# A decoder step on one core: the entry of the gate stage, with its first weights loaded earlier and one gate block kept out of memory

## The chip, the cores and the metric

The kernel is one program on one core of a Trainium2 chip. Its time is the device time of one execution in microseconds (us); of several runs the median counts. The engines that matter are TensorE (PE, matrix products; PEld are its weight loads), VectorE (DVE), ScalarE (ACT) and GpSimd (POOL). SyncE (SP) issues most transfers, and the transfers themselves are carried by the DMA engines. Each engine works through its own instructions in order and waits for others at semaphores.

## The reference, cut to what matters

One decoder layer for 1024 prompt tokens and 8 x 4 sample tokens, T = 1056 columns in all, with a model width of 1024, in float32:

```python
h = rmsnorm(x, w['norm1_g'])
proj = h @ w['w_in']
a_uv, pool_in, qkv, f_raw, z, xbc, dt_raw, gate_raw = jnp.split(proj, split_points, axis=-1)
...        # four branches: gated MLP y_a, pooling y_b, attention y_c, state scan y_d (256 wide each)
merged = jnp.zeros_like(x)
for i, y_i in enumerate((y_a, y_b, y_c, y_d)):
    gate = jax.nn.sigmoid(gate_raw[..., i * D_MODEL:(i + 1) * D_MODEL])
    merged = merged + gate * (y_i.astype(adt) @ w['w_branch'][i])
x = x + merged @ w['w_out']
...        # then a convolved feed-forward layer and the final norm
```

Branch D is a chunked scan over the prompt, with a carried state, and one stored state for each of the 8 sample sequences (`ssd_chunked`, called with `h0`). Its output goes through a norm before it is merged.

## The kernel before, in words

Everything is kept transposed: 128 channels on the partitions, the 1056 tokens along the free side, in three chunks of 352. A product is done in three parts for precision: each operand is split into a high part (a copy rounded to the matmul's type) and a low part (the rest), and high x high, low x high and high x low are summed. One block of 128 output channels over an input of 1024 is 8 steps x 3 parts x 3 chunks = 72 matmuls. Weights are loaded by SP into two buffers `w_raw`, and GpSimd splits each block (`split`, L897: a mark, a copy to `w_hi`, a subtraction to `w_lo`). The y tensors are split by ScalarE (`y_hi`) and VectorE (`y_lo`).

The stretch that the change touches runs like this.

*Early gate blocks.* The gates of branches 0 and 1 (16 blocks, `NE`) are computed in pieces of 9 matmuls between the small matmuls of the attention (6 blocks), of the scan (8 blocks) and of the sample states (2 blocks, `STATE_FILL` = 2 pieces for each of 8 states). TensorE sums a block in PSUM buffer `ps[1]`; ScalarE copies it out and stores it to `gate_raw` in device memory (L1178, L1179). The gates of branches 2 and 3 are computed later, one block each per merge round.

*The scan.* In step c of 9, VectorE multiplies the decays into the score matrix (`seg`, L1756), TensorE uses it (L2306), VectorE takes the results, and then prepares the decays of the next step (L1730, L1732). GpSimd does the step's state products (the last is `xte`, L961) and then the split of a weight block. After the decays of the last step VectorE makes 16 copies into `ctm` (L1782), which the sample states' matmuls read.

*The sample states.* For each of 8 states: GpSimd makes a masked copy (`xtm`, L970, in the buffers `c_s` and `nc_s`), TensorE multiplies it (L2352), transposes the next old state (L2343), does the filling pieces (L2144) and the outputs (L2362). VectorE builds the new state (L1743); SP then loads the state after next (L756) and stores the new one (L758).

*The merge stage.* In round j of 8, for 128 output channels: a gate block of branch 2, branches 0 and 2 (18 matmuls each, L2408), a gate block of branch 3, branches 1 and 3. The order of branches is `BRANCHES` = (0, 2, 1, 3), and their sums lie in `ps` 1, 0, 0, 1. Gates of branches 0 and 1 are loaded back from `gate_raw` into `sgl` (which lies in `cst`) and get their sigmoid there (L1274); those of 2 and 3 get it from PSUM into `sg` (L1283). VectorE multiplies and adds (L1818, L1820). In round 0 the first gate block is interleaved with the transposes of branch D's nine tiles (L2379), which VectorE moves out (L1803). The memory of the scan is then free (`free_of_s1`), and only then may the branch weights be loaded and `y_hi` and `y_lo` be written, in the order of the channels 0 to 7 (L1287, L1809).

The weights of round 0 come late in SP's order: behind the loads and stores of all states,

```python
        sp.wait_ge(h_sent[0], 16 * 5)
        sp.wait_ge(h_sent[1], 16 * 4)
...
        load_gate_weights(0, 0)
        load_gate_weights(0, 1)
        free_of_s1(sp)
```

Of the kernel before, what the change touches and what calls it, by code (L numbers as in the profile page):

```python
# [22 lines left out]
F32 = mybir.dt.float32  # L23
# [6 lines left out]
P = 128  # L30
# [18 lines left out]
FH = 2  # L49
NE = 16  # L50
EA = 6
# [117 lines left out]
def decoder_layer(nc, a, o):  # L169

    top = ExitStack()
    gate_raw = nc.dram_tensor("gate_raw", (NE, P, T), F32, kind="Internal").ap()

# [3 lines left out]
    def sem(name):  # L177
        return top.enter_context(nc.semaphore(name))
# [93 lines left out]
    N1B = len(JOBS)  # L272
    early = [("eg", g, COL_GATE + (g % 2) * D + (g // 2) * P) for g in range(NE)]
    JOBS += early[:EA]
# [19 lines left out]
    ATT_FILL = [(1, 1) if qb < NT // 2 else (1, 0) for qb, h in steps]  # L294
    SSD_LEAD, SSD_FILL, STATE_FILL = 2, [(3, 3)] + [(4, 4)] * (NT - 1), 2

# [212 lines left out]
    ld_sg, sl_ready = sem("ld_sg"), sem("sl_ready")  # L509
    BRANCHES, BRANCH_PS = (0, 2, 1, 3), (1, 0, 0, 1)  # L510
    merged_used = sem("merged_used")
    EARLY_H2 = 2
# [11 lines left out]
    y_sent = [sem(f"y_sent{n}") for n in range(3)]  # L524
    W3 = N1F
    W4 = W3 + 2 * KD
# [79 lines left out]
    def _(sp):  # L606
# [142 lines left out]
        for c in range(NT):  # L749
            load_early(ssd_blocks[c][1])  # L750

        for b in range(NB + 2):
            if b >= 2:
                sp.wait_ge(h_ready, b - 1)
            if b < NB:
                sp.dma_start(h0[b % 2][:, :, :], by_pair(a["state_ssd"][0, b])).then_inc(ld_h0[b % 2], 16)  # L756
            if b >= 2:
                sp.dma_start(by_pair(o["ssd_sample"][0, b - 2]), h_out[b % 2]).then_inc(h_sent[b % 2], 16)  # L758
# [21 lines left out]
        def load_gate_weights(j, s):  # L780

            load_block(W3, s, 2, j, w_in[:, :, bass.ds(at(j * P + (COL_GATE + (2 + s) * D)), P)])

        load_gate_weights(0, 0)
        load_gate_weights(0, 1)
        free_of_s1(sp)
        for n in range(2):
            sp.wait_ge(e_sent[n], 16 * (NE // 2))
        load_branch(0, 0)
        load_branch(0, 1)  # L790
        load_gate(0, 0)
        with sp.Fori(1, KD) as j:
# [87 lines left out]
    def _(gp):  # L880
# [85 lines left out]
        for b in range(NB):  # L966
            split_early(state_blocks[b - 1] if b >= 1 else ssd_blocks[-1][1])
            if b >= 2:
                pt_filled(gp, ("sn", b - 2))
            od.run(g.tensor_scalar(xtm[b % 2][:, :], xte[NT % 2][0:NS].rearrange("p h d -> p (h d)"),  # L970
                                   const("bsel", slice(0, NS), slice(b, b + 1)), None, ALU.mult), xtm_done)

        def split_block(base, q, per, i):
# [5 lines left out]
        def split_gate(j, s):  # L979

            gp.wait_ge(gate_full, j * 2 + (s - 1))
            split_block(W3, s, 2, j)

# [9 lines left out]

        gp.wait_ge(e_full, NE - 1)
        split_block(W3, 0, 2, 0)
        gp.wait_ge(e_full, NE)
        split_block(W3, 1, 2, 0)
        free_of_s1(gp)
        split_branch(0, 0)
        split_branch(0, 1)  # L1000
        od.peel()
        with gp.Fori(1, KD) as j:
# [63 lines left out]
    def _(act):  # L1066
# [104 lines left out]
        def evacuate_early(blocks):  # L1171

            nonlocal n_early
            while n_early < blocks:
                act.wait_ge(e_full, n_early + 1)
                if n_early >= 2:
                    act.wait_ge(e_sent[n_early % 2], 16 * (n_early // 2))
                od.run(sc.activation(in_chunks(gst[n_early % 2]), chunked(1), ACT.Copy), (e_free, n_early + 1))  # L1178
                act.dma_start(gate_raw[n_early], gst[n_early % 2]).then_inc(e_sent[n_early % 2], 16)  # L1179
                n_early += 1  # L1180
# [90 lines left out]
        def gate_loaded(j, s):  # L1271

            act.wait_ge(ld_sg, j * 32 + 16 * (s + 1))
            od.run(sc.activation(sgl, sgl, ACT.Sigmoid), sl_ready)  # L1274
# [10 lines left out]
        free_of_s1(act)  # L1285
        for b in range(KD):
            od.run(sc.activation(y_hi[:, b, :], y_all[:, b, :], ACT.Copy), y_hi_done)  # L1287
        od.peel()
        gate_loaded(0, 0)
        gate_computed(0, 0)  # L1290
        gate_loaded(0, 1)
        gate_computed(0, 1)
        with act.Fori(1, KD) as j:
            od.enter(j, 1)
            gate_loaded(j, 0)
            gate_computed(j, 0)
            gate_loaded(j, 1)
            gate_computed(j, 1)
# [110 lines left out]
    def _(dve):  # L1409
# [339 lines left out]
        for c in range(NT + 1):  # L1749
# [25 lines left out]
            if c + 1 <= NT:  # L1775
                decays(c + 1)
            if c == NT - 1:

                dve.wait_ge(d_zeroed, 1)
                for g in range(2):  # L1780
                    for b in range(NB):
                        od.run(v.tensor_copy(ctm[:, g, b, b * NQ:(b + 1) * NQ], xc[:, 4 + g, SEQ + b * NQ:SEQ + (b + 1) * NQ]),  # L1782
                               ctm_done)
                for b in range(NB):
                    new_state(b)
# [10 lines left out]
        for t in range(NT + 1):  # L1796
            r = rows_of(t)
            key = ("yd", t)
            if t == 0:
                for n in range(2):  # L1800
                    dve.wait_ge(e_sent[n], 16 * (NE // 2))
            pt_filled(dve, key)
            od.run(v.tensor_tensor(y_all[:, 6:8, t * P:t * P + r],  # L1803
                                   pt_of(key)[:, 0:256].rearrange("p (b t) -> p b t", b=2)[:, :, 0:r],
                                   pv[:, PV_SG:PV_SG + 2].unsqueeze(2).to_broadcast([P, 2, r]), ALU.mult), ptf_of(key))

        for b in range(KD):
            dve.wait_ge(y_hi_done, b + 1)
            od.run(v.tensor_tensor(y_lo[:, b, :], y_all[:, b, :], y_hi[:, b, :].bitcast(F32), ALU.subtract), y_split)  # L1809
# [138 lines left out]
    def _(pe):  # L1948
# [433 lines left out]
        def gate(j, s, between=None):  # L2382
            n = W3 + s
            pe.wait_ge(w_split, j * 2 + (n + 1))
            if isinstance(j, int) and s == 0:
                pe.wait_ge(ps0_free, NST + NT + 1)
            else:
                pe.wait_ge(br_read, j * 4 + (2 * s - 1))
            product(ps[s], n % 2, between).then_inc(gate_full, 1)

        def branch(j, p):
            q = BRANCHES[p]
            pe.wait_ge(b_split, j * 4 + (p + 1))
            if isinstance(j, int):
                pe.wait_ge(y_split, 2 * q + 2)
            if p % 2 == 1:
                pe.wait_ge(sg_ready, j * 2 + (p // 2 + 1))
            elif p == 2:
                pe.wait_ge(br_read, j * 4 + 2)
            elif isinstance(j, int):  # L2400
                pe.wait_ge(e_free, NE)
            else:
                pe.wait_ge(br_read, j * 4)
# [8 lines left out]
        def merge_round(j, between=None):  # L2412
            gate(j, 0, between)
            branch(j, 0)
            branch(j, 1)
            gate(j, 1)
            branch(j, 2)
            branch(j, 3)
# [168 lines left out]
```

## Time and profile before

| | us |
|---|---|
| runs shown | 1977.64, 1973.81, 1972.26 |
| their median | 1973.81 |
| the profiled execution's own time | 1970.56 |
| its span, from first to last instruction | 1968.8 |
| TensorE busy in it | 1870.7 (95%) |
| VectorE busy | 892.4 (45%) |
| ScalarE busy | 412.1 (21%) |
| GpSimd busy | 575.3 (29%) |

The profile is of one execution. TensorE is busy almost always, and 88% of the chain of work that ended last is TensorE's. So the time is what TensorE has to do, at the clock that it is granted, and the gaps in which it waits. The waits list who waited for whom; the timeline lists instructions in the order of time, and in brackets behind a row is the idle time before it and what ended it.

### The profile page before, as it was taken

To read this page: it belongs to the slowest core of one execution; us is meant where nothing else is said; L and a number is where in the kernel's file an instruction comes from. 1 tells how busy PE (TensorE), PEld (TensorE's weight loads), DVE (VectorE), ACT (ScalarE), POOL (GpSimd) and SP (SyncE) were. 2 spreads that over 40 slices of the span, in tenths; PEclk is the share of its full clock that TensorE was granted. 3 is DMA by queue.
4 is the path that set the end of the run, shared out by engine and by line. 5 is a ranking of instruction groups with operands and counts; after the bars stand their busy time and mean duration, and the time that the engine had idled before them with its cause. 6 is when DMAs were issued, how large, how long until landed. Compare 5 with 4: busy or idle time off the path is not lost.

```text
span 1968.8 us, 29869 instructions
## 1 busy us (share of the span) xinstructions
PE 1870.7 (95%) x11562; PEld 1795.2 (91%) x11562; DVE 892.4 (45%) x1359; ACT 412.1 (21%) x591; POOL 575.3 (29%) x532
## 2 busy tenths in 40 slices
PE   5899899999999878999999999999999999999997
PEld 4899887888899868999999989999999999999986
DVE  5763334435533325222232255555555554555555
ACT  5211123423411112111121132112111111111223
POOL 2223211022233323333331223324323432432420
PEclk9899999999999889999999999999999999999998
DMA  4121311012222122222223311112111111111202
GB/s 123 45 52 38 87 45 44 12 60 65 60 65 68 55 78 68 70 80 81 81 62 85 98 44 44 43 33 64 43 32 53 44 41 43 53 43 32 64 11 97
DMA packets 156098, 113.44 MB, mean 58 GB/s; under 512 B 10742, under 2 KB 146651, under 8 KB 155990
## 3 DMA queue, kind: packets, MB, share of 16 engines
q1 hardware_dynamic: 153084, 102.61, 18.4%
q10 hardware_dynamic: 2940, 9.81, 1.3%
q8 instruction: 51, 0.84, 0.2%
q14 instruction: 23, 0.19, 0.0%
HBM read 95.37 MB, written 16.99 MB: 57 GB/s over the span
## 4 chain that ended last, share of the span: by engine, by line
PE 88%; DVE 7%; ACT 1%; DMA 1%; issue 1%; POOL 1%; ACTq 0%; SPq 0%; DVEq 0%; POOLq 0%
PE ps L1959 17%; PE ps L1965 16%; PE ps L1962 16%; PE ps L2144 10%; PE ps L2408 4%; PE pt L2505 4%; PE pt L2507 4%; PE pt L2506 4%; PE ps L2188 2%; PE ps L2126 2%; PE ps L2445 1%; PE pt L2176 1%; DVE y_lo L1809 1%; DMA w_raw<-in_w_in 1%; DVE ext L1863 1%
## 5 line engine op out<-in xcount | busy, mean ns | idle before, releaser
L1959 PE MATMUL ps<-h_hi,w_hi 128*128 128x352 f32 x2088 | 458.7, 328 | 26.6 <-POOL w_lo L901 16.8
L1965 PE MATMUL ps<-h_hi,w_lo 128*128 128x352 f32 x2088 | 452.5, 324 | 0.0
L1962 PE MATMUL ps<-h_lo,w_hi 128*128 128x352 f32 x2088 | 452.0, 325 | 0.0
L1959 PEld LDWEIGHTS ps<-h_hi,w_hi 128*128 128x128 f32 x2088 | 355.2, 190 | 29.9 <-POOL w_lo L901 17.5
L894 POOL TENSOR_TENSOR mark<-eps 128x1 f32<-128x1 f32 x159 | 44.4, 279 | 1134.3 <-PE ps L1965 503.0
L1965 PEld LDWEIGHTS ps<-h_hi,w_lo 128*128 128x128 f32 x2088 | 360.2, 189 | 0.0
L1962 PEld LDWEIGHTS ps<-h_lo,w_hi 128*128 128x128 f32 x2088 | 357.0, 189 | 0.0
L901 POOL TENSOR_TENSOR w_lo<-w_raw,w_hi 128x1024 fp32r<-128x1024 f32 x127 | 332.4, 2617 | 10.2
L1897 DVE TENSOR_TENSOR y_all<-y_all,pt 128x352 f32<-128x352 f32 x264 | 137.5, 521 | 113.8 <-PE pt L2507 110.9
L2505 PE MATMUL pt<-act_hi,w_hi 128*128 128x352 f32 x528 | 172.4, 327 | 7.4 <-DVE y_all L1897 6.9
L2507 PE MATMUL pt<-act_hi,w_lo 128*128 128x352 f32 x528 | 170.6, 323 | 0.0
L2506 PE MATMUL pt<-act_lo,w_hi 128*128 128x352 f32 x528 | 170.0, 322 | 0.0
L1877 DVE SCALAR_TENSOR_TENSOR cv<-ext,pv,cv 128x1072 f32<-128x1072 f32 x88 | 144.7, 1644 | 11.9 <-DVE cv L1877 0.2
L900 POOL CAST w_hi<-w_raw 128x1024 fp32r<-128x1024 f32 x127 | 132.9, 1046 | 0.0
L1353 ACT ACTIVATE cv<-ext,pv 128x1072 f32<-128x1072 f32 x44 | 56.5, 1285 | 305.6 <-DVE ext L1866 305.6
L2505 PEld LDWEIGHTS pt<-act_hi,w_hi 128*128 128x128 f32 x528 | 99.3, 188 | 11.7 <-DVE y_all L1897 10.7
L2506 PEld LDWEIGHTS pt<-act_lo,w_hi 128*128 128x128 f32 x528 | 99.4, 188 | 0.0
L2507 PEld LDWEIGHTS pt<-act_hi,w_lo 128*128 128x128 f32 x528 | 99.1, 188 | 0.0
L1863 DVE TENSOR_TENSOR ext<-ps,cst 128x704 f32<-128x704 f32 x44 | 39.2, 892 | 125.4 <-PE ps L1965 125.2
L1363 ACT ACTIVATE act_hi<-cv 128x1024 fp32r<-128x1024 f32 (+1 forms) x44 | 28.4, 645 | 310.1 <-DVE cv L1883 309.4
L2144 PE MATMUL ps<-h_hi,w_hi 128*128 128x352 f32 x384 | 90.1, 343 | 0.2 <-ACT y_all L1178 0.2
L2144 PE MATMUL ps<-h_lo,w_hi 128*128 128x352 f32 x384 | 84.6, 329 | 0.0
(341 smaller groups left out, 2112.5 us busy)
## 6 DMA issues: line engine op xcount, KB each, us to landing
w_raw<-in_w_in SPq DMA_DIRECT2D x52, 512.0 KB, 4.2
w_raw<-in_ffn_up SPq DMA_DIRECT2D x44, 512.0 KB, 3.9
w_raw<-in_ffn_down SPq DMA_DIRECT2D x22, 512.0 KB, 3.6
gate_raw<-y_all ACTq DMA_DIRECT2D x16, 528.0 KB, 2.7
cst<-gate_raw SPq DMA_DIRECT2D x16, 528.0 KB, 3.6
x_tok<-in_x_prompt SPq DMA_DIRECT2D x8, 512.0 KB, 4.1
bw_raw<-in_w_branch SPq DMA_DIRECT2D x32, 128.0 KB, 3.5
w_raw<-in_w_out SPq DMA_DIRECT2D x8, 512.0 KB, 5.0
```

The costliest lines, as they stand in the source:

```text
L900: od.run(g.tensor_copy(hi, raw))
L901: od.run(g.tensor_tensor(lo, raw, hi.bitcast(F32), ALU.subtract), w_split)
L1877: od.run(v.scalar_tensor_tensor(cv[k][:, 0:w], x[:, j:j + w], pv[:, bass.ds(blk + (PV_FW + 2 * NFF * j), 1)], cv[k][:, 0:w], ALU.mult, ALU ...
L1897: od.run(v.tensor_tensor(dst, dst, pt[n % 2][:, 0:CH], ALU.add), dn_done)
L1959: mm(dst[:, c, 0:CH], f_hi[n][:, k, :], h_hi[:, k, tok], start=k == 0, stop=False)
L1962: mm(dst[:, c, 0:CH], f_hi[n][:, k, :], h_lo[:, k, tok], start=False, stop=False)
L1965: last = mm(dst[:, c, 0:CH], f_lo[n][:, k, :], h_hi[:, k, tok], start=False, stop=k == KD - 1)
L2144: last = mm(ps[1][:, c, 0:CH], w[n % 2][:, k, :], h[:, k, c * CH:(c + 1) * CH], start=k == 0 and m == 0, stop=k == KD - 1 and m == 2)
L2408: last = mm(ps[BRANCH_PS[p]][:, c, 0:CH], w[p % 2][:, k, :], y[:, 2 * q + k, c * CH:(c + 1) * CH], start=k == 0 and n == 0, stop=k == 1 an ...
L2505: mm(dst, w[:, m, :], act_hi[:, k, tok], start=k == 0, stop=False)
L2506: mm(dst, w[:, m, :], act_lo[:, k, tok], start=False, stop=False)
L2507: last = mm(dst, w_rest[:, m, :], act_hi[:, k, tok], start=False, stop=k == 1)
```

## The change

Five edits belong together:

1. The weights of the first gate block of branch 2 and of one gate block of branch 0 are loaded before the sample states' loads (SP), and split among and right behind the masked copies (GpSimd). The weights of the first gate block of branch 3 follow behind the states.
2. One of the 16 early gate blocks (the first of branch 0) is no longer computed among the states and stored. There are 15 early blocks, and each state has one filling piece in place of two. The kept block is computed in round 0 behind the first gate block, summed in `ps[1]`, and ScalarE takes its sigmoid straight from there. The early blocks are now in the order branch 1, 0, 1, ... 
3. GpSimd's masked copies no longer stand behind a split: a split now stands behind the second of them.
4. VectorE's 16 copies into `ctm` move from the last scan step to step 2, behind the decays of step 3.
5. `y_hi` and `y_lo` are written in the order of the branches (channels 0, 1, 4, 5, 2, 3, 6, 7). Behind the first four, ScalarE does the sigmoids of the first gate block and of the kept block, then the last four.

```diff
-NE = 16
+NE = 15
...
-    early = [("eg", g, COL_GATE + (g % 2) * D + (g // 2) * P) for g in range(NE)]
+    early = [("eg", g, COL_GATE + ((g + 1) % 2) * D + ((g + 1) // 2) * P) for g in range(NE)]
...
-    SSD_LEAD, SSD_FILL, STATE_FILL = 2, [(3, 3)] + [(4, 4)] * (NT - 1), 2
+    SSD_LEAD, SSD_FILL, STATE_FILL = 2, [(3, 3)] + [(4, 4)] * (NT - 1), 1
...
+    Y_ORDER = [2 * q + k for q in BRANCHES for k in range(2)]
...
-    W3 = N1F
+    W3 = N1F + 1
...
+        for n, col in ((N1F, COL_GATE + 2 * D), (N1F + 1, COL_GATE)):
+            load_block(n, 0, 2, 0, w_in[:, :, col:col + P])
+
         for b in range(NB + 2):
...
-        load_gate_weights(0, 0)
         load_gate_weights(0, 1)
         free_of_s1(sp)
...
         load_branch(0, 0)
         load_branch(0, 1)
-        load_gate(0, 0)
...
         for b in range(NB):
-            split_early(state_blocks[b - 1] if b >= 1 else ssd_blocks[-1][1])
             if b >= 2:
                 pt_filled(gp, ("sn", b - 2))
             od.run(g.tensor_scalar(xtm[b % 2][:, :], xte[NT % 2][0:NS].rearrange("p h d -> p (h d)"),
                                    const("bsel", slice(0, NS), slice(b, b + 1)), None, ALU.mult), xtm_done)
+            if b == 1:
+                split_job(N1F)
...
-        gp.wait_ge(e_full, NE - 1)
-        split_block(W3, 0, 2, 0)
-        gp.wait_ge(e_full, NE)
-        split_block(W3, 1, 2, 0)
+        split_job(N1F + 1)
         free_of_s1(gp)
         split_branch(0, 0)
         split_branch(0, 1)
+        split_gate(0, 1)
+        gp.wait_ge(e_full, NE + 1)
...
-        for b in range(KD):
+        for n, b in enumerate(Y_ORDER):
+            if n == 4:
+                gate_computed(0, 0)
+                act.wait_ge(e_full, NE + 1)
+                od.run(sc.activation(in_chunks(sgl), chunked(1), ACT.Sigmoid), sl_ready)
             od.run(sc.activation(y_hi[:, b, :], y_all[:, b, :], ACT.Copy), y_hi_done)
-        od.peel()
-        gate_loaded(0, 0)
-        gate_computed(0, 0)
         gate_loaded(0, 1)
         gate_computed(0, 1)
...
-            if c == NT - 1:
-
+            if c == 2:
                 dve.wait_ge(d_zeroed, 1)
                 for g in range(2):
                     for b in range(NB):
                         od.run(v.tensor_copy(ctm[:, g, b, b * NQ:(b + 1) * NQ], xc[:, 4 + g, SEQ + b * NQ:SEQ + (b + 1) * NQ]),
                                ctm_done)
+            if c == NT - 1:
                 for b in range(NB):
                     new_state(b)
...
-        for b in range(KD):
-            dve.wait_ge(y_hi_done, b + 1)
+        for n, b in enumerate(Y_ORDER):
+            dve.wait_ge(y_hi_done, n + 1)
...
         def merge_round(j, between=None):
             gate(j, 0, between)
+            if isinstance(j, int):
+                pe.wait_ge(w_split, N1F + 2)
+                pe.wait_ge(e_free, NE)
+                product(ps[1], (N1F + 1) % 2).then_inc(e_full, 1)
             branch(j, 0)
```

In round 0 the first branch now waits for the kept block's sigmoid (`sl_ready`), and each branch for the first y blocks in the new order. The other lines of the diff adjust counts.

GpSimd at the entry of the sample states, before: the last state product, a split, and the first two masked copies.

```order
L961 TENSOR_TENSOR xte<-xdt,dec 32x256
L894 TENSOR_TENSOR mark<-eps 128x1
L900 CAST w_hi<-w_raw 128x1024
L901 TENSOR_TENSOR w_lo<-w_raw,w_hi 128x1024
L970 TENSOR_SCALAR c_s<-xte,cst 32x256
L970 TENSOR_SCALAR nc_s<-xte,cst 32x256
```

The same place in the changed kernel:

```order
L963 TENSOR_TENSOR xte<-xdt,dec 32x256
L971 TENSOR_SCALAR c_s<-xte,cst 32x256
L971 TENSOR_SCALAR nc_s<-xte,cst 32x256
L896 TENSOR_TENSOR mark<-eps 128x1
L902 CAST w_hi<-w_raw 128x1024
L903 TENSOR_TENSOR w_lo<-w_raw,w_hi 128x1024
```

The split (now of the first gate block's weights) stands behind two masked copies, and ahead of the third.

VectorE in scan step 2 and at the start of step 3, before (buffer numbers are shown):

```order
L1771 TENSOR_TENSOR zt<-zt,xd0 128x256
L1772 ISA yoff,stat<-zt 128x256
L1730 TENSOR_TENSOR dec1<-ps0,sdt_t 128x4
L1732 SCALAR_TENSOR_TENSOR seg1<-ps0,sdt_t,cst 128x128 x4
L1756 TENSOR_TENSOR seg1<-seg1,ps0 128x512
```

The same place in the changed kernel:

```order
L1775 TENSOR_TENSOR zt<-zt,xd0 128x256
L1776 ISA yoff,stat<-zt 128x256
L1734 TENSOR_TENSOR dec1<-ps0,sdt_t 128x4
L1736 SCALAR_TENSOR_TENSOR seg1<-ps0,sdt_t,cst 128x128 x4
L1786 COPY stg1<-xc 128x4 x16
L1760 TENSOR_TENSOR seg1<-seg1,ps0 128x512
```

The 16 copies (`stg1` is the memory of `ctm`) now stand between the decays of step 3 and the product that TensorE reads in that step.

ScalarE at the entry of the merge stage, before:

```order
L1269 ACT_TABLE_LOAD
L1269 ACTIVATE stat<-stat,eps 128x9
L1287 ACTIVATE y_hi<-y_all 128x1056 x8
L1274 ACT_TABLE_LOAD
L1274 ACTIVATE cst<-cst 128x1056
L1283 ACTIVATE sg<-ps 128x1056
```

The same place in the changed kernel:

```order
L1271 ACT_TABLE_LOAD
L1271 ACTIVATE stat<-stat,eps 128x9
L1293 ACTIVATE y_hi<-y_all 128x1056 x4
L1285 ACT_TABLE_LOAD
L1285 ACTIVATE sg<-ps 128x1056
L1292 ACTIVATE cst<-ps 128x1056
L1293 ACTIVATE y_hi<-y_all 128x1056 x4
```

The eight copies are cut in two, and the sigmoids of the first gate block and of the kept block stand between.

## Rows read from the trace of the kernel before

**Rows 1.** Waits of TensorE, 215 to 1100 us: total, times, longest.

```profile
PE ps L1959 <- POOL w_lo L901: 12.3, 1, 12.3
PE pt L2352 <- POOL c_s L970: 7.2, 1, 7.2
PE ps L2408 <- POOL bw_lo L991: 4.5, 1, 4.5
...
PE ps L2408 <- ACT sg L1283: 1.4, 1, 1.4
...
PE ps L1959 <- DVE y_all L1818: 1.3, 1, 1.3
...
PE pt L2343 <- ACT h0t L1265: 0.9, 1, 0.9
```

**Rows 2.** Table by stretches: length, busy time of each engine, PEclk, DMA share.

```profile
681.70:688.80 7.10, 7.07 (x25) 6.47 (x26) 1.66 (x8) 0.38 (x1) 1.86 (x2) 0.51 0.13 39
...
734.60:739.90 5.30, 5.30 (x18) 5.30 (x19) 0.00 (x0) 0.00 (x0) 3.53 (x3) 0.50 0.00 0
...
755.50:760.60 5.10, 5.04 (x18) 5.04 (x18) 5.00 (x4) 5.01 (x5) 4.60 (x6) 0.52 0.05 15
```

**Rows 3.** Timeline of VectorE, scan and entry of the states: start, us, what.

```profile
596.88 1.50 DVE L1732 SCALAR_TENSOR_TENSOR seg<-ps,sdt_t,cst 128x128 f32<-128x128 f32 x4
...
599.68 0.69 DVE L1756 TENSOR_TENSOR seg<-seg,ps 128x512 f32<-128x512 f32 x1 [1.30 <-ACT seg L1255]
...
675.58 7.17 DVE L1782 COPY stg<-xc 128x4 f32<-128x4 f32 x16
```

**Rows 4.** Timeline of TensorE, scan step 3.

```profile
602.90 1.00 PE L2306 MATMUL ps<-xdt,seg 128*128 128x64 f32 x8
```

**Rows 5.** Instructions of line 1782: ns shortest, median, longest.

```profile
L1782 DVE COPY stg<-xc x16: 169/204/2189, 675.6 to 682.5; 128x4 f32<-128x4 f32 x16
```

**Rows 6.** Timeline of GpSimd, entry of the states.

```profile
676.33 0.62 POOL L961 TENSOR_TENSOR xte<-xdt,dec 32x256 f32<-32x256 f32 x1
...
678.29 2.35 POOL L901 TENSOR_TENSOR w_lo<-w_raw,w_hi 128x1024 fp32r<-128x1024 f32 x1
680.74 0.94 POOL L970 TENSOR_SCALAR c_s<-xte,cst 32x256 f32<-32x256 f32 x1
```

**Rows 7.** Timeline of TensorE, one of the states.

```profile
693.25 0.62 PE L2362 MATMUL ps<-h0t,stg 128*32 128x128 f32 x4
...
694.63 0.73 PE L2144 MATMUL ps<-h_hi,w_hi 128*128 128x352 f32 x3
...
697.69 0.62 PE L2362 MATMUL ps<-h0t,stg 128*32 128x128 f32 x4
```

**Rows 8.** Tile h, loads of the old states: from issue to landing.

```profile
DMA to landing us min/median/max: 2.1/2.2/4.3
```

**Rows 9.** Timeline of VectorE, entry of the merge stage.

```profile
722.46 0.41 DVE L1767 TENSOR_TENSOR yoff<-ps,eacs 32x256 f32<-32x256 f32 x1
...
725.09 3.44 DVE L1795 TENSOR_SCALAR zt<-zt,stat 128x256 f32<-128x256 f32 x9
...
751.00 14.35 DVE L1809 TENSOR_TENSOR y_lo<-y_all,y_hi 128x1056 fp32r<-128x1056 f32 x8 [1.27 <-ACT y_hi L1287]
```

**Rows 10.** Timeline of ScalarE, entry of the merge stage.

```profile
749.81 8.90 ACT L1287 ACTIVATE y_hi<-y_all 128x1056 fp32r<-128x1056 f32 x8 [25.25 <-DVE y_all L1803]
```

**Rows 11.** Instructions of tile y_lo: ns shortest, median, longest.

```profile
L1809 DVE TENSOR_TENSOR y_lo<-y_all,y_hi x8: 1257/1568/3334, 751.0 to 762.0; 128x1056 fp32r<-128x1056 f32 x8
```

**Rows 12.** Timeline of TensorE after two short waits elsewhere.

```profile
240.59 0.46 PE L2126 MATMUL ps<-k_a,q_a 66*128 66x128 f32 x2 [2.57 <-ACT stg L1168]
...
242.28 1.08 PE L2144 MATMUL ps<-h_hi,w_lo 128*128 128x352 f32 x3
...
1159.14 0.77 PE L1959 MATMUL ps<-h_hi,w_hi 128*128 128x352 f32 x3 [3.58 <-DVE h_lo L1853]
...
1160.59 1.08 PE L1965 MATMUL ps<-h_hi,w_lo 128*128 128x352 f32 x3
```

More of the change, by code:

```diff
@@ L171, in decoder_layer @@
     top = ExitStack()
-    gate_raw = nc.dram_tensor("gate_raw", (NE, P, T), F32, kind="Internal").ap()
+    gate_raw = nc.dram_tensor("gate_raw", (NE + 1, P, T), F32, kind="Internal").ap()
     def sb(scope, name, shape, dt=F32):
@@ L787, in _ @@
         for n in range(2):
-            sp.wait_ge(e_sent[n], 16 * (NE // 2))
+            sp.wait_ge(e_sent[n], 16 * ((NE + 1 - n) // 2))
         load_branch(0, 0)
         load_branch(0, 1)
-        load_gate(0, 0)
         with sp.Fori(1, KD) as j:
@@ L979, in split_gate @@
         def split_gate(j, s):
-            gp.wait_ge(gate_full, j * 2 + (s - 1))
+            gp.wait_ge(gate_full, j * 2 + s if isinstance(j, int) else j * 2 + (s - 1))
             split_block(W3, s, 2, j)
@@ L1178, in evacuate_early @@
                 od.run(sc.activation(in_chunks(gst[n_early % 2]), chunked(1), ACT.Copy), (e_free, n_early + 1))
-                act.dma_start(gate_raw[n_early], gst[n_early % 2]).then_inc(e_sent[n_early % 2], 16)
+                act.dma_start(gate_raw[n_early + 1], gst[n_early % 2]).then_inc(e_sent[n_early % 2], 16)
                 n_early += 1
@@ L1271, in gate_loaded @@
         def gate_loaded(j, s):
-            act.wait_ge(ld_sg, j * 32 + 16 * (s + 1))
+            act.wait_ge(ld_sg, j * 32 + 16 * s)
             od.run(sc.activation(sgl, sgl, ACT.Sigmoid), sl_ready)
@@ L1285, in _ @@
         free_of_s1(act)
-        for b in range(KD):
+        for n, b in enumerate(Y_ORDER):
[3 more added lines that the diff above has]
+                od.run(sc.activation(in_chunks(sgl), chunked(1), ACT.Sigmoid), sl_ready)
             od.run(sc.activation(y_hi[:, b, :], y_all[:, b, :], ACT.Copy), y_hi_done)
-        od.peel()
-        gate_loaded(0, 0)
-        gate_computed(0, 0)
         gate_loaded(0, 1)
         gate_computed(0, 1)
+        od.peel()
         with act.Fori(1, KD) as j:
-            od.enter(j, 1)
+            od.enter(j, 1, [(sl_ready, 2), (sg_ready, 2)])
             gate_loaded(j, 0)
@@ L1800, in _ @@
                 for n in range(2):
-                    dve.wait_ge(e_sent[n], 16 * (NE // 2))
+                    dve.wait_ge(e_sent[n], 16 * ((NE + 1 - n) // 2))
             pt_filled(dve, key)
@@ L2383, in gate @@
             n = W3 + s
+            if isinstance(j, int) and s == 0:
+                n = N1F
             pe.wait_ge(w_split, j * 2 + (n + 1))
@@ L2394, in branch @@
             if isinstance(j, int):
-                pe.wait_ge(y_split, 2 * q + 2)
+                pe.wait_ge(y_split, 2 * p + 2)
             if p % 2 == 1:
@@ L2400, in branch @@
             elif isinstance(j, int):
-                pe.wait_ge(e_free, NE)
+                pe.wait_ge(sl_ready, 1)
             else:
```

## The prediction

> **What bounds the kernel now.** I read the waits of TensorE first. The reader is to see that the stretch between the state scan and the second gate block holds the waits that this change can touch: 12.3 us for the first gate weights, 7.2 us for the first masked copy of the sample states, 4.5 us for the first branch weights, and 1.4, 1.3 and 0.9 us on smaller things [rows 1]. Their sum is 27.6 us. After them TensorE loops over gate and branch blocks nearly without a gap, so what is won before the second gate block should reach the end.
>
> Second, the table by stretches: after three of these waits TensorE works at the lower of its two clocks, 1.2 GHz, for 7.07, 5.30 and 5.04 us of busy time [rows 2]. About half of that is lost, 8.7 us; I take 8, since some small matmuls of the states are in it. So 35.6 us of that stretch are not work. The work itself neither shrinks nor grows: one gate block of 72 matmuls moves from the states to behind the first gate block.
>
> Third, three timelines of the changed places, used below.
>
> **The change, part by part.** In each sum, times are those of the trace of before, as if everything earlier stood still.
>
> *State scan.* The sixteen small copies to `ctm` now stand on VectorE between the decays of step 3 and its `seg` product. The decays end at 598.4 us and the product starts at 599.68 and takes 0.69; TensorE reads it at 602.90 [rows 3, 4]. One copy takes 0.204 us in the median, but 2.189 at most [rows 5]: a copy that meets a running GpSimd operation ends with that operation. In step 3 GpSimd runs the state product, then the two halves of a split, as it did beside these copies in the old place, where all 16 took 7.17 us [rows 3] with two masked copies in the way as well. I count eight copies up to the end of the split (603.4) and eight free ones, ending at 605.1; the product is there at 605.8, so TensorE waits 3.0 us. Bounds: 16 free copies (3.3 us) end with the product at 602.4, no wait; 7.2 us give 3.4 us. I take 3.0, since the same split lies there.
>
> The Trainium skill (SBUF — State Buffer, Who interferes with whom) has a rule that speaks against this move: VectorE and GpSimd share a port pair, and whichever operation starts first holds it until it ends. The trace agrees, in the 2.189 us copy, and by the rule the wait is 3.0 us; without it there would be none.
>
> *Entry of the states.* GpSimd did a weight split of 3.7 us between the last state product (ends 676.95) and the first masked copy (starts 680.74, 0.94 us) [rows 6]. Now the copy follows the product and is done at 678.0. TensorE, idle since 674.5, waits 3.5 us in place of 7.2. The copies on VectorE, which held the new states back until 682.75 [rows 3], are gone from here. The next split now starts behind the second masked copy, from 679.1 to 682.7; the third copy, behind it, comes at 683.7, just when TensorE wants it.
>
> *States.* Each of 8 states loses one piece of 9 matmuls. Before, a state took 1.38 us for outputs and state matmuls and 3.06 for two pieces, 4.44 in all [rows 7]. Now 2.9. What could be late is the state's own reload: from its product on TensorE, 0.8 us on VectorE, the load (2.2 us median, 4.3 at most [rows 8]) and small change, so 3.2 us until the state after next can be turned; TensorE comes to that turn some 3 us after the product. I add 0.5 us over all; bounds 0 and 6 (eight states at the slowest landing). The two weight loads now go ahead of the state loads on SP's queue; the second waits for a split that ends at 665.8, so the first two states are asked for 8 us before use, and 4.3 us cover them.
>
> *First gate block.* Its weights are split by 683, and it starts at 678.0 + 8 x 2.9 + 1.1 for the last scan product and the waits, about 702.5, so the 12.3 us go. Next late is the read of the last scan result on VectorE, which ended at 722.87 [rows 9], 0.57 us after TensorE had stopped (its wait of 12.3 us ended at 734.6 [rows 1, 2]): 0.6 us. Inside the block TensorE turns branch D's tiles, from the fourth piece on. VectorE scales the nine tiles for 3.44 us [rows 9] and only then empties the turned ones; it also starts late, since the split of the kept block's weights lies beside it for 2.4 us. I get a wait of 1.8 us before the third turn, between 0 and 3.4 us (all of the scaling).
>
> *Kept gate block.* Its 72 matmuls (some 12 us, by 18 in 3.06) now stand before the first branch and cover the branch weights' load and split and the first y splits: 4.5 and 1.4 us go. ScalarE takes its sigmoid straight from PSUM, and TensorE waits for that, since the first branch writes the same buffer: one activation of this size is 8.90/8 = 1.1 us [rows 10]; I take 1.2.
>
> *The added wait.* ScalarE waits for the kept block with the last four `y_hi` copies queued behind. VectorE needs all eight for `y_lo`, and only then does its first merge, which TensorE's second gate block waits for. From the end of the kept block: sigmoid to 1.15; two branches on TensorE to 7.0 (18 matmuls, 2.9 us each); `y_hi` five to eight from 1.15, ready at 2.25 to 5.6. GpSimd splits the next gate weights at that time, its long half from 1.3 to 3.65; a free `y_lo` is 1.26 us, the slowest took 3.33 [rows 11], beside a split. So four `y_lo` run from 3.65 to 8.8, the merge to 10.1: a wait of 3.1 us. Bounds: 1.7 without that meeting, 3.7 at the pace of all eight of before (14.35 us [rows 9]).
>
> *Clock.* The three new waits of about 3 us have nothing like them in this stretch before. Elsewhere a wait of 2.57 us and one of 3.58 were both followed by triples of matmuls of 1.08 us [rows 12], the pace of 1.2 GHz: at 2.4 GHz six triples run in 3.06 [rows 7]. The second kept on so for some 3.4 us, a loss of 1.7. Bounds 0 and 3.5 (half of the 7.07 us); I take 1.7 for each, 5.1.
>
> Sum of what comes: 3.0 + 3.5 + 0.5 + 0.6 + 1.8 + 1.2 + 3.1 + 5.1 = 18.8 us. What goes: 27.6 + 8 = 35.6. Gain 16.8 us. The new order of the gate blocks and the missing store and load of 528 KB lie beside TensorE's work and are costed at nothing; if the load were not covered in the loop, each round would show it, and none does.
>
> The profiled execution has a span of 1968.8 and a time of 1970.56 us; the sum gives 1953.8. The median of the runs is 1973.81, 3.2 higher, and gives 1957.0. I predict 1955.
>
> **Rivals.**
>
> *The clock stays up* (16%). The three waits stay short enough, or fall so that the clock is not touched: gain 21.9, about 1950. For it: waits of 1.4 and 1.3 us left it at 2.4 GHz. Against: no row with 2.5 us or more did.
>
> *The states become bound by their transfers* (12%). With one piece per state there is little to cover a slow landing. At 4.3 us each, two states take (5.3 + 2.2) us, 3.75 a state in place of 2.9: 6 us, so about 1961. For it: the 0.9 us wait already shows this chain once with two pieces. Against: the median of 2.2.
>
> *It doesn't do what it says* (4%): the first gate still waits, for a load or split that is late. Then the 12.3 us stay, the gain is 4.5, about 1968. Against: 20 us lie between that split and its use.
>
> *Slower* (4%). The states run one after another at the pace of the state's round trip, since the new loads and stores crowd them out. It decides from where the loss passes 16.8 us: 2.1 us a state more, 5 us a state, so 2 x 5 - 2.2 - 1.0, a landing of 6.8 us. At 10 us it would be 6.6 us a state, 30 us lost, 1985. The slowest landing seen is 4.3.
>
> **How the numbers follow.** The forecast has 64%. Runs of this kernel tell about 0.3%, 5.9 us, from no change. All cases but the last two are faster by more than that; of the forecast and the transfer case I leave 2% for none. Faster 0.90, same 0.06, slower 0.04. Range: from 1946 (clock up and no wait in the scan) to 1964 (slow landings and a late sigmoid).
>
> **What would show it.** Right: no wait on `w_lo` before the first gate block; a new wait of about 3 us on `seg` in the scan at step 3; a wait of about 3.5 us before the first masked product; states every 2.9 us; one wait of about 1.2 us before the first branch and about 3 us before the second gate block, on the merge. Wrong: states at 3.7 us or more, a first gate block later than 25 us after the first masked product, or longer waits in the loop from the second round on.

## The result and the profile after

The changed kernel takes 1962.57 us (median of 5 runs, 1961.23 to 1968.48); runs of the kernel before beside it took 1975.85 (1972.26 to 1977.64). The ratio is 0.9948 with a 95% interval of 0.9929 to 0.9966: 0.5% faster by the ratio, some 10 us (the two medians lie 13.3 apart), where 16.8 (the sum) to 18.8 us (1955 against 1973.81) were forecast. The time lies inside the range, but by the ratio the gain is little more than half of the one predicted. The profiled execution took 1961.23 us with a span of 1959.5; the sum had given 1953.8 for its time.

The waits of TensorE in the trace after, in total, times and longest, answer to [rows 1]:

```profile
PE pt L2356 <- POOL c_s L971: 3.4, 1, 3.4
PE ps L1963 <- DVE y_all L1822: 3.1, 1, 3.1
...
PE ps L2310 <- DVE seg L1760: 2.7, 1, 2.7
...
PE pt L2347 <- DMA h<-in_state_ssd: 2.0, 1, 2.0
...
PE ps L2414 <- ACT cst L1292: 1.3, 1, 1.3
PE pt L2383 <- DVE y_all L1807: 1.2, 1, 1.2
...
PE ps L1963 <- DVE yoff L1771: 0.7, 1, 0.7
```

The 12.3 us on the first gate weights and the 4.5 us on the branch weights are gone. Six of the seven waits that came were forecast to within 0.6 us (3.5, 3.1, 3.0, 1.2, 1.8 and 0.6). The seventh, 2.0 us on a reload of the old states, was forecast at 0.5.

The clock answers to [rows 2]. The table by stretches of the trace after (length, TensorE's busy time, granted clock, DMA share, GB/s) covers scan step 3, the first four states, the last four, the first gate block with the kept one, and the second gate block. A granted clock of 1.00 is 2.4 GHz, and 0.50 is 1.2 GHz:

```profile
603.80:621.00 17.20, 17.20 (x104) 0.90 0.14 50
680.50:700.30 19.80, 17.73 (x77) 0.68 0.19 54
700.30:714.00 13.70, 12.92 (x85) 1.00 0.20 62
714.10:742.70 28.60, 26.07 (x162) 1.00 0.24 67
751.90:766.30 14.40, 14.39 (x72) 0.79 0.32 93
```

The lower clock lies in three places, behind the 2.7, the 3.4 and 2.0, and the 3.1 us waits. In the states it comes twice, as TensorE's timeline shows (start, duration, what, and in brackets the idle time before). A triple, three matmuls merged into one row (x3), takes 1.08 us at 1.2 GHz and 0.64 at 2.4:

```profile
680.54 1.22 PE L2356 MATMUL pt<-xb,c_s 32*128 32x128 f32 x4 [3.43 <-POOL c_s L971]
...
683.06 1.08 PE L2148 MATMUL ps<-h_lo,w_hi 128*128 128x352 f32 x3
...
685.94 0.88 PE L2356 MATMUL pt<-xb,nc_s 32*128 32x128 f32 x4
...
689.14 0.71 PE L2356 MATMUL pt<-xb,c_s 32*128 32x128 f32 x4
691.87 0.44 PE L2347 MATMUL pt<-cst,h 128*128 128x128 f32 x2 [2.02 <-DMA h<-in_state_ssd]
692.06 0.73 PE L2148 MATMUL ps<-h_hi,w_hi 128*128 128x352 f32 x3
...
695.08 1.22 PE L2356 MATMUL pt<-xb,nc_s 32*128 32x128 f32 x4
...
697.59 1.08 PE L2148 MATMUL ps<-h_lo,w_hi 128*128 128x352 f32 x3
...
700.27 0.71 PE L2356 MATMUL pt<-xb,c_s 32*128 32x128 f32 x4
...
703.27 0.71 PE L2356 MATMUL pt<-xb,nc_s 32*128 32x128 f32 x4
```

From one masked product to the next a state takes 5.40, 3.20, 5.94, 5.19 and then 3.00 us. Against 3.0 at full clock, and without the 2.02 us wait, that is 2.4 + 0.2 = 2.6 us lost to 1.2 GHz behind the entry wait (3.43 us, before the first masked product) and 0.9 + 2.2 = 3.1 behind the reload wait (2.02 us), 5.7 in all.

To compare kernels I use one stretch: from TensorE's first product of the scan (`ps<-xdt,seg`, 557.55 us before, 555.61 after) to its third gate block, where the loop over the other rounds begins (784.32 and 772.15). It holds all of TensorE's work that the change moves. Before it takes 226.8 us and after 216.5, so the change is worth 10.2 us there; the forecast was 16.8.

### The profile page after: what moved, and what is told of

The parts are those of the page before. It is cut to its first block, busy times and chain, and to the rows that moved or that the text cites. A ratio compares the mean times of both kernels' runs of the same rounds, so it can differ in the third digit from the quotient of the medians.

```text
span 1959.5 us, 29866 instructions
## 1 busy us (share of the span) xinstructions
PE 1872.4 (96%) x11562; PEld 1796.6 (92%) x11562; DVE 891.0 (45%) x1359; ACT 410.9 (21%) x590; POOL 573.0 (29%) x532
## 4 chain that ended last, share of the span: by engine, by line
PE 88%; DVE 8%; ACT 2%; issue 1%; DMA 1%; ACTq 0%; POOL 0%; SPq 0%; DVEq 0%; POOLq 0%
PE ps L1963 17%; PE ps L1969 17%; PE ps L1966 16%; PE ps L2148 9%; PE ps L2414 4%; PE pt L2515 4%; PE pt L2517 4%; PE pt L2516 4%; PE ps L2192 2%; PE ps L2130 2%; PE ps L2455 1%; PE pt L2180 1%; DVE ext L1867 1%; PE ps L2103 0%; PE ps L2020 0%
## 5 line engine op out<-in xcount | busy, mean ns | idle before, releaser
L1963 PE MATMUL ps<-h_hi,w_hi 128*128 128x352 f32 x2112 | 464.7, 328 | 16.8 <-POOL w_lo L903 4.4
L1969 PE MATMUL ps<-h_hi,w_lo 128*128 128x352 f32 x2112 | 457.5, 324 | 0.0
L1963 PEld LDWEIGHTS ps<-h_hi,w_hi 128*128 128x128 f32 x2112 | 360.0, 190 | 20.1 <-issue 9.2
L1966 PEld LDWEIGHTS ps<-h_lo,w_hi 128*128 128x128 f32 x2112 | 361.3, 189 | 0.0
L903 POOL TENSOR_TENSOR w_lo<-w_raw,w_hi 128x1024 fp32r<-128x1024 f32 x127 | 331.5, 2610 | 10.2
```

Source lines behind the costliest of these rows:

```text
L903: od.run(g.tensor_tensor(lo, raw, hi.bitcast(F32), ALU.subtract), w_split)
L1963: mm(dst[:, c, 0:CH], f_hi[n][:, k, :], h_hi[:, k, tok], start=k == 0, stop=False)
L1966: mm(dst[:, c, 0:CH], f_hi[n][:, k, :], h_lo[:, k, tok], start=False, stop=False)
L1969: last = mm(dst[:, c, 0:CH], f_lo[n][:, k, :], h_hi[:, k, tok], start=False, stop=k == KD - 1)
```

## The experiments

"Stretch" is the one just named, read in each trace. The "states" run from the first masked product to the first gate block. "vs before" is the ratio with its 95% interval.

| kernel | median us | vs before | stretch us | states us |
|---|---|---|---|---|
| before | 1972 to 1976 | 1 | 226.8 | 52.9 |
| changed | 1962.57 | 0.9948 (0.9929 to 0.9966) | 216.5 | 33.6 |
| e0 changed, again | 1960.98 | 0.9935 (0.9920 to 0.9951) | 216.9 | 33.9 |
| e1 entry filled | 1958.75 | 0.9927 (0.9907 to 0.9948) | 206.1 | 25.8 |
| e2 late sigmoid | 1956.30 | 0.9912 (0.9890 to 0.9934) | 211.5 | 34.2 |
| e3 copies spread | 1957.36 | 0.9917 (0.9901 to 0.9932) | 211.5 | 33.1 |
| e4 third buffer | 1956.34 | 0.9907 (0.9890 to 0.9924) | 208.4 | 28.2 |
| e5 early weights alone | 1960.32 | 0.9931 (0.9908 to 0.9954) | 211.8 | 40.3 |
| e7 copies back | 1959.17 | 0.9930 (0.9912 to 0.9948) | 209.1 | 31.7 |
| e9 early weights, split later | 1956.16 | 0.9906 (0.9889 to 0.9922) | 208.8 | 40.9 |
| e6 four edits | 1944.76 | 0.9850 (0.9830 to 0.9869) | 197.0 | 24.4 |
| e8 four edits, pieces dealt again | 1945.91 | 0.9861 (0.9840 to 0.9882) | 195.3 | 22.9 |

Runs of one kernel spread over 4.5 to 13.4 us, and the profiled executions reach the scan, through unchanged code, between 555.5 us (e0) and 563.8 us (e1). So whole times tell these kernels apart only roughly, and I go by the stretch, of which there is one trace for each kernel and two for the changed one. (In e1, e6 and e8 two pieces, 3.1 us, lie ahead of the states; in before, e5 and e9 the states hold a gate block of 12 us more.)

**e0, the changed kernel again.**

> The changed kernel once more, unaltered. In its first trace TensorE stood 12.2 us ahead of the kernel before at the start of the output projection (1020 against 1032) and 12.2 ahead at 1908, but only 9.3 at the end: in the tail, whose code is the same in both, a wait of 2.22 us was followed by matmuls at 1.2 GHz, which did not happen in the trace of before. Theory A (the clock's loss behind a short wait is part of this kernel's timing and comes back in every execution): the same place again, profile within 1 us of 1961.2, ratio 0.994 to 0.996. Theory B (where the clock falls differs from execution to execution): other places, the profile up to 3 us off the first, the ratio up to 0.15% away from 0.9948. In the states both expect 2 us on the reload and two stretches at 1.2 GHz if they belong to the change.

The states repeat: 2.22 us on the reload, lower clock twice, stretch 216.9. The unchanged code doesn't: the drop in the tail did not come back, but from the output projection to the end of the feed-forward blocks TensorE took 2.4 us longer. The profiled time, 1960.81, is the one that A named, but only because these two differences nearly cancel. So B holds for where the clock falls in the rest of the kernel, and a gain is better read from the stretch than from the end.

**e1, the entry filled.** Two of the eight pieces ahead, none in the last two states.

```diff
+    STATE_LEAD, STATE_FILL = 2, (1, 1, 1, 1, 1, 1, 0, 0)
         turn_state(0)
+        fill(STATE_LEAD)
-            fill(STATE_FILL)
+            fill(STATE_FILL[b])
```

> Two of the eight filling pieces of the states stand ahead of the first state product, and states 7 and 8 have none. The entry wait of 3.4 us becomes about 0.4, since two pieces take 3.1 us. Theory A (clock): without that wait TensorE goes into the states at 2.4 GHz, the 3.3 us lost there at 1.2 GHz go too, so against the changed kernel -3.0 - 3.3 = -6.3 us, and up to -9 if the second drop goes as well; about 1953 to 1956. Rival (transfers): the states wait for their reloads; TensorE now comes to them earlier and with less to do in states 7 and 8, so the 3 us come back as waits for the load or for ScalarE's copy: 0 to -2 us, 1960 to 1963.

The timeline of TensorE at the same place:

```profile
687.11 0.71 PE L2358 MATMUL pt<-xb,c_s 32*128 32x128 f32 x4 [0.56 <-POOL c_s L972]
...
688.51 0.64 PE L2149 MATMUL ps<-h_lo,w_hi 128*128 128x352 f32 x3
...
690.12 0.71 PE L2358 MATMUL pt<-xb,nc_s 32*128 32x128 f32 x4
691.14 0.44 PE L2348 MATMUL pt<-cst,h 128*128 128x128 f32 x2 [0.31 <-DMA h<-in_state_ssd]
```

The entry wait is 0.56 us in place of 3.43, triples take 0.64 in place of 1.08, states 3.0 to 3.4 us from the start (the whole of 687.1 to 707.0 at a granted clock of 1.00), and no reload wait is above 0.31. From the first masked product to the first gate block it takes 25.8 us, 7.7 less, of which 3.1 are the two pieces moved ahead into a wait. Waits of 0.94 and 0.85 us come instead in the last two states, which have no piece. The stretch falls by 10.4; the rest comes from other places: the scan wait of 2.66 us was here not followed by the lower clock (1.6), and the last one by less of it (1.2). For the entry, theory A holds: with its wait, its lower clock (2.6 us) is gone. But no load landed later than 2.3 us in this trace, where one took 4.0 in the changed kernel. So the reload wait and the clock behind it, some 5 us in the changed kernel, may be gone for that reason and not for the filled entry, and the transfer rival was not put to a late load here. The median, 1958.75, lies between the two theories' times; the profiled execution had reached the scan 8.2 us later than that of the changed kernel.

**e2, the late sigmoid.**

```diff
             if n == 4:
                 gate_computed(0, 0)
-                act.wait_ge(e_full, NE + 1)
-                od.run(sc.activation(in_chunks(sgl), chunked(1), ACT.Sigmoid), sl_ready)
             od.run(sc.activation(y_hi[:, b, :], y_all[:, b, :], ACT.Copy), y_hi_done)
+        act.wait_ge(e_full, NE + 1)
+        od.run(sc.activation(in_chunks(sgl), chunked(1), ACT.Sigmoid), sl_ready)
```

> ScalarE's wait for the kept gate block and its sigmoid stand behind all eight copies to y_hi in place of behind the fourth. The copies five to eight then end at about 740, before the kept block does (741.4), so the sigmoid comes no later. Theory A: the wait of 3.1 us on the first merge goes (the last y_lo end at about 744, the merge follows the first branch), and the 2.7 us that TensorE lost at 1.2 GHz behind it go with it: -5.8 us against the changed kernel, about 1956. Rival 1 (the wait is not the copies' but the split's or the gate's): 0 us. Rival 2 (the clock falls all the same, since 1.3 us of wait stay ahead of the first branch): -3 us, about 1959.5.

```profile
749.65 0.72 PE L1963 MATMUL ps<-h_hi,w_hi 128*128 128x352 f32 x3 [0.25 <-DVE y_all L1822]
750.20 0.64 PE L1966 MATMUL ps<-h_lo,w_hi 128*128 128x352 f32 x3
```

The second gate block waits 0.25 us in place of 3.14 and runs at full clock: 11.7 us to its first branch in place of 14.4. The stretch is 5.0 us shorter, 5.6 without the slightly longer states. Theory A; both rivals fall.

**e3, the copies spread.**

```diff
-            if c == 2:
+            if c == 0:
                 dve.wait_ge(d_zeroed, 1)
+            if c < NT:
                 for g in range(2):
-                    for b in range(NB):
-                        od.run(v.tensor_copy(ctm[:, g, b, b * NQ:(b + 1) * NQ], xc[:, 4 + g, SEQ + b * NQ:SEQ + (b + 1) * NQ]),
+                    od.run(v.tensor_copy(ctm[:, g, c, c * NQ:(c + 1) * NQ], xc[:, 4 + g, SEQ + c * NQ:SEQ + (c + 1) * NQ]),
```

> The sixteen small copies of step 3 are spread: two behind the decays of each of the eight steps. Two copies take 0.4 to 4.4 us; a step has some 3 us of slack on VectorE. Theory A: the wait of 2.7 us on seg in step 3 goes and some 2 us at 1.2 GHz with it: -4.5 us, about 1957.5. Rival (each pair meets a running GpSimd operation and ends with it): eight waits of up to 1 us in its place, no gain or a loss of up to 5 us, 1962 to 1967.

No wait on `seg` is left, the step behind it takes 15.6 us in place of 17.25, and the stretch is 5.0 us shorter, 4.5 of them in the scan. In VectorE's timeline a pair takes 0.37 us, since it falls where GpSimd stands idle (598.88 to 599.66 us):

```profile
597.49 1.51 DVE L1736 SCALAR_TENSOR_TENSOR seg<-ps,sdt_t,cst 128x128 f32<-128x128 f32 x4
599.03 0.37 DVE L1785 COPY stg<-xc 128x4 f32<-128x4 f32 x2
600.29 0.69 DVE L1760 TENSOR_TENSOR seg<-seg,ps 128x512 f32<-128x512 f32 x1 [0.88 <-ACT seg L1257]
```

In the changed kernel all sixteen took 6.43 us there. Theory A holds.

**e4, a third buffer for the loaded states.**

```diff
-            if b >= 2:
-                sp.wait_ge(h_ready, b - 1)
+            if 3 <= b < NB:
+                sp.wait_ge(h_ready, b - 2)
             if b < NB:
-                sp.dma_start(h0[b % 2][:, :, :], by_pair(a["state_ssd"][0, b])).then_inc(ld_h0[b % 2], 16)
+                sp.dma_start(h0[b % 3][:, :, :], by_pair(a["state_ssd"][0, b])).then_inc(ld_h0[b % 3], 16)
             if b >= 2:
+                sp.wait_ge(h_ready, b - 1)
```

> A third buffer for the loaded sample states, so that each load is asked for one state earlier. The entry wait of 3.4 us stays as it is. Read from the trace: the changed stretch, from the first product of the scan (L2310) to the third gate block on TensorE, 216.5 and 216.9 us in the two traces of the changed kernel. Theory A (each wait of some 2 us or more brings the lower clock back): the reload wait of 2.0 us goes, and with it the second drop to 1.2 GHz in the states, 3.3 us: the stretch takes 211 to 212. Rival 1 (the second drop is the entry wait's own, and would come anyway): 214.5. Rival 2 (the load's slow landing of 4.0 us moves with it and only hits another state): 216 to 217.

```profile
686.32 1.22 PE L2358 MATMUL pt<-xb,c_s 32*128 32x128 f32 x4 [3.44 <-POOL c_s L973]
...
691.72 0.85 PE L2358 MATMUL pt<-xb,nc_s 32*128 32x128 f32 x4
```

The entry wait is 3.44 as in the changed kernel, the reload wait is gone, and the lower clock ends within the second state's masked product. The states take 28.2 us in place of 33.6: 5.4 less, where A said 5.3. (The rest of the 8.2 us is again the clock behind the scan wait and the last one, 1.6 and 1.2.) So the second drop belonged to the reload wait, not to the entry. One load landed late here too, after 3.7 us, and no wait came of it: rival 2 falls as well.

**e5, the early weights alone, on the kernel before.**

```diff
+        load_block(W3, 0, 2, 0, w_in[:, :, COL_GATE + 2 * D:COL_GATE + 2 * D + P])
         for b in range(NB + 2):
...
-        load_gate_weights(0, 0)
...
+            if b == 5:
+                gp.wait_ge(e_full, NE - 1)
+                gp.wait_ge(ld_w[W3 % 2], 16 * (W3 // 2 + 1 + (1 - W3 % 2)))
+                split(w_raw[W3 % 2][:, :, :], w_hi[W3 % 2][:, :, :], w_lo[W3 % 2][:, :, :])
...
-        split_block(W3, 0, 2, 0)
```

> The kernel before with one part of the change alone: the first gate weights are loaded ahead of the sample states and split after the sixth masked product; two pieces per state, no kept block, copies and y order as before. Theory A (the kept block is what pays, by covering the branch weights): the 12.3 us before the first gate block go, but the branch weights still come only after the last stores, so their wait grows from 4.5 to some 11 us; the stretch goes from 226.8 to 220 to 223. Rival (the early weights alone do it, and the rest of the change only costs): 212 to 215, no worse than the changed kernel's 216.5.

My theory A was wrong here; the rival was near (212 to 215 said, 211.8 measured). The waits of TensorE:

```profile
PE pt L2355 <- POOL c_s L971: 7.2, 1, 7.2
PE ps L2411 <- POOL bw_lo L996: 4.5, 1, 4.5
PE ps L2411 <- ACT sg L1286: 2.1, 1, 2.1
```

The wait for the branch weights stays 4.5 us and doesn't grow, since their loads and splits come some 10 us earlier too. So this part alone is worth 15.0 us on the stretch, more than the whole change with its 10.2.

**e7, the copies put back** to where they stood, in an otherwise changed kernel.

```diff
-            if c == 2:
+            if c == NT - 1:
                 dve.wait_ge(d_zeroed, 1)
```

> The changed kernel with the sixteen small copies put back to where they stood, behind the decays of the last step. Theory A: the wait of 2.7 us in step 3 and 1.65 us of clock go, but the copies now hold back the new states by 3.3 to 7.2 us, on which the reload of the third state and so TensorE hang: entry plus reload wait 3 to 6 us longer, the stretch 215 to 219: the move gains or costs nothing within 2 us. Rival (the copies hide behind the entry wait of 3.4 us): 212.

The rival was nearer, and even it expected too small a gain: 209.1. The entry wait is 3.5 us either way, the copies (7.20 us beside GpSimd) hold TensorE for 0.40 and 0.17 us, and the reload wait is 1.5:

```profile
686.93 0.44 PE L2346 MATMUL pt<-cst,h 128*128 128x128 f32 x2 [1.46 <-DMA h<-in_state_ssd]
...
688.03 1.08 PE L2147 MATMUL ps<-h_lo,w_hi 128*128 128x352 f32 x3
```

So the lower clock came back behind 1.46 us too. The stretch is 7.4 us shorter: 4.4 in the scan (2.7 of wait, 1.65 of clock), 1.85 in the states, and 1.2 from the clock behind the last wait. That last part is not this edit's, since it moved in e1 and e4 too; nor did the scan's wait bring its 1.65 there. What is surely gained by undoing the edit is 2.7 + 1.85, some 4.5 us.

**e6 and e8, four edits together** (e1 to e4), e8 with the pieces dealt 2 ahead, then 1, 1, 1, 1, 0, 1, 0, 1.

> Four edits on the changed kernel together: copies spread over the steps (measured -5.0 us on the stretch), the kept block's sigmoid behind all copies (-5.0), two filling pieces ahead of the first state product (-7.7), and the third buffer for the loaded states (some 0.8 us of short waits for loads). Theory A (the terms add up, since each takes away its own wait with its own lower clock): the stretch takes 198 to 200 us, the kernel some 1944 to 1948. Rival (what is won falls to waits that lay hidden, or the clock falls elsewhere): 204 or more.

> The four edits together, with the eight filling pieces dealt otherwise: two ahead of the first state product, then one in states 1 to 4, 6 and 8. The last piece again lies in the last state, so ScalarE no longer empties it ahead of a state's copy. Theory A (each wait near the first gate block costs itself and the clock behind it): the waits of 0.94 and 0.85 us at the end of the states go or fall to half, and with them part of the 1.9 us at 1.2 GHz in the first gate block: the stretch 194 to 196 us in place of 197.0. Rival (a state with no piece waits for its own copies wherever it stands): 197 to 198.

The terms add up: 18.5 us by e6's expectation, 19.5 measured. The stretch falls to 197.0 and to 195.3 us, as theory A had it for e8 (194 to 196). One load landed after 3.9 us in e6 and 3.7 in e8, and with the third buffer no reload wait came of it. In e8 only four waits of 0.6 to 1.3 us are left in the stretch, and its granted clock is 1.00 from 560 to 755 us:

```profile
PE ps L2418 <- ACT cst L1296: 1.3, 1, 1.3
PE pt L2387 <- DVE y_all L1810: 1.2, 1, 1.2
PE ps L1966 <- DVE yoff L1774: 0.7, 1, 0.7
PE pt L2360 <- POOL c_s L974: 0.6, 1, 0.6
```

Both are faster than either kernel: 1.5% and 1.4% against the kernel before. The 1.7 us between them are below what whole times can tell.

**e9, early weights with the last early split moved later**, on the kernel before.

```diff
-            split_early(state_blocks[b - 1] if b >= 1 else ssd_blocks[-1][1])
...
+            if b == 1:
+                split_early(NE)
```

> The kernel before with the early weights (first part of the change) and with GpSimd's last early split moved behind the second masked product; still two pieces per state, no kept block, small copies and y order as before. It lacks what the changed kernel adds beyond these: the kept block, the y order, the moved copies. The early weights alone gave 211.8 us on the stretch. Theory A (the kept block covers 4.5 us of branch weights, but thins the states, and is worth nothing net): the entry wait goes from 7.2 to 3.5, with as much of the lower clock as before: 207 to 209, better than the changed kernel's 216.5. Rival (the copies on VectorE then hold back the states, and the kept block is needed): 212 or more.

The stretch takes 208.8 us: theory A holds. e7 (209.1) adds the kept block and the y order to the same two edits. By these two traces the additions are worth nothing net: they remove 3.4 us for the branch weights and 3.5 for a gate, and pay with thinner states and waits of 3.2, 1.5, 1.3 and 1.2 us.

## Why the prediction was right and wrong

*What goes* was right: none of the 12.3, 7.2, 4.5, 1.4, 1.3 and 0.9 us waits of [rows 1] is left as it was, and in the first gate block and the first two branches no lower clock is left. Their sum and the 8 us of clock were read rightly.

*The waits that come* were right, all but one. Scan 2.7 (3.0 said), entry 3.4 (3.5), last scan result 0.7 (0.6), turns 1.2 (1.8), kept block 1.3 (1.2), second gate block 3.1 (3.1). The copies took 6.43 us beside the split, against the free 3.3 of [rows 5]; they ended 0.2 us earlier than the forecast had them, and the merge before the second gate block came behind four `y_lo` that began beside the split, as it said.

*The step that failed is the term "Clock"*: "I take 1.7 for each, 5.1". The lower clock came four times and not three, and three of the four drops cost more. Behind the scan wait it was 1.65 us, as said. Behind the entry wait it was 2.6, behind the last wait 2.7 (14.4 us against 11.7 in e2), and behind the reload wait, which had no price, 3.1. The sum is 10.1, 5.0 more than forecast. I had priced only the three waits that I had listed, each from one row of [rows 12], though my bound for each was 3.5, and had not asked what a further wait in the thinned states would bring. e4 shows it: with the load in time, that drop is gone.

*The term "states"* was the second: 0.5 us for late reloads, inside bounds of 0 to 6, measured 2.0 in one wait. A state takes 3.0 us and not 2.9, 0.8 over eight: I had halved the 3.06 us of two pieces [rows 7], but one piece alone takes 1.62 (701.10 to 702.72 us in the trace after). e4 shows wait and drop together: with the reload in time 5.4 us go.

Together 5.0 + 1.5 + 0.8 = 7.3, less 0.9 for the turns and the scan, which came out better, is 6.4 of the 6.5 us that the stretch was longer than forecast (226.8 - 16.8 = 210.0 against 216.5). The remaining 1 us to the end lies in unchanged code: the profiled execution reached the scan 1.9 us earlier than that of before and lost 2.9 in the tail.

*The rivals.* "The states become bound by their transfers" named the time well (1961), but by luck: one landing was slow, not all eight, and most of the shortfall is the clock. "The clock stays up" was wrong in this kernel; in e8 the clock stayed up, but only because the waits of about 3 us were gone. Its argument that waits of 1.4 and 1.3 us left the clock at 2.4 GHz does not carry over: in e7 a wait of 1.46 us, with two of 0.40 and 0.17 shortly ahead of it, was followed by 1.2 GHz.

*Not seen at all:* that the moved copies need not move. The forecast gave them 3.0 us of wait, and 1.7 of the clock, as a cost, and took for granted that they had to leave the entry; e7 shows that the entry's own 3.5 us cover them but for 0.6 us (0.40 and 0.17).

## What to carry to other kernels

A forecast wait on TensorE is to be entered with its clock, as a range (here 0 to 3.1 us a wait), and beside it the next wait that a slowed TensorE or a thinner filling will bring; here the clock cost 10.1 us against 14.4 of waits. Filling is worth most where TensorE would stand still: two pieces moved from the end of the states to their entry took 2.9 us of wait and 2.6 of clock off the entry, against new waits of 0.94 and 0.85 us at the end (e1). And a change of several parts is to be priced part by part, each against the others' covers: the early weights alone gave 15.0 us, the rest took 5 back.

## What the runs showed of the hardware

**A slow load has a packet of code beside it.** In the changed kernel the load of the fourth state, issued at 687.80, landed after 4.0 us, in place of 2.0 to 2.3 for the five others. The transfer view of 687 to 690 us, and of 680 to 687 with an ordinary one (queue: packets, MB, share; then issues with KB and us to landing):

```profile
q1 hardware_dynamic: 510, 0.25, 27.6%
q8 instruction: 1, 0.02, 3.5%
issues: line engine op xcount, KB each, median us to landing
h<-in_state_ssd SPq DMA_DIRECT2D x1, 128.0 KB, 4.0
```

```profile
q1 hardware_dynamic: 544, 0.26, 12.7%
issues: line engine op xcount, KB each, median us to landing
h<-in_state_ssd SPq DMA_DIRECT2D x1, 128.0 KB, 2.1
```

A single packet of 0.02 MB on the instruction queue lay beside the slow one. Twelve traces hold 8 loads, issued within the states, that landed after 3.3 to 4.4 us; each had such a packet 0.6 to 2.2 us behind its issue. All others landed in 2.0 to 2.3 us, and four of those had one too: three 2.1 to 2.3 us behind, at the end of their data, and one in the trace of before, 1.6 us behind. That load landed after 2.1 us all the same, but the store issued 0.4 us after it took 3.7, where the four before it took 2.1 to 2.5. In the changed kernel, e0, e2 and e3 it is the fourth state's load each time. That the packet is the cause was not tried apart from this. The Trainium skill (Advanced Engine Details and Errata, ISA Cache) gives 16 KB as the line of the instruction cache; the 51 packets of that queue in the trace after, 0.84 MB in all, are 16.5 KB each and agree.

**The same wait doesn't always lower the clock.** The scan wait of 2.66 to 2.67 us was followed by 1.2 GHz in the traces of the changed kernel (twice) and e2, and not in e1 and e4. The three reached the scan at 555.5 to 555.6 us, the two at 563.0 and 563.8; whether that has to do with it is not shown. In the tail, whose code is the same in all twelve, a wait of 2.2 us was followed by matmuls at half pace in the traces after and e5, and at full pace in the other ten. First the trace after, then that of before:

```profile
1932.14 0.64 PE L2515 MATMUL pt<-act_hi,w_hi 128*128 128x352 f32 x1 [2.22 <-DVE y_all L1901]
1932.58 0.49 PE L2516 MATMUL pt<-act_lo,w_hi 128*128 128x352 f32 x1
```

```profile
1942.99 0.43 PE L2505 MATMUL pt<-act_hi,w_hi 128*128 128x352 f32 x1 [2.23 <-DVE y_all L1897]
1943.26 0.32 PE L2506 MATMUL pt<-act_lo,w_hi 128*128 128x352 f32 x1
```

So one such wait costs 0 to 3.1 us of clock. What decides it between two executions stays open. Over the unchanged part from the output projection to the last feed-forward block, traces of these kernels differ by up to 4.3 us (882.8 to 887.1), and ahead of the scan by up to 8.3, which is why a gain of 5 us hardly shows in one whole time.
